# A two-layer decoder trunk on one core: the first weight block by halves, the variance product later, another order of the first value products, and more idle products

## The chip, the core and the metric

The kernel runs on one core of one Trainium2 chip. The metric is the device time of one execution in microseconds (us). Five engines work side by side, each on its own stream of instructions, and wait for each other by semaphores: TensorE (PE in the profile, its weight loads PEld), VectorE (DVE), ScalarE (ACT), GpSimd (POOL) and SyncE (SP), which here only issues DMAs.

## The reference

The input x has 512 tokens of 1024 numbers. Layer 0 is RMSNorm, one input projection, an attention of 8 heads with dilated windows beside a causal convolution of width 31 over 512 channels (its result goes through a LayerNorm over the channels and a swish), one output projection, a residual, and a mixture of experts. Layer 1 is RMSNorm, a retention of 4 heads (queries and keys 256 wide, values 512), its output projection, a residual and another mixture of experts. All of it is float32.

```python
u = rms_norm(h, mix_norm[layer])
h = h + mixer(u)                      # layer 0: attention + convolution; layer 1: retention
h = h + hierarchical_moe(rms_norm(h, ffn_norm[layer]), ...)   # top 2 of 32 experts, hidden 512
...
mu = jnp.mean(yf, axis=-1, keepdims=True)                     # LayerNorm of the convolution
var = jnp.mean(jnp.square(yf - mu), axis=-1, keepdims=True)
```

## The kernel before

**Products by parts.** Each float32 product of the projections is made of three products of a faster format: the high part of the data with the high part of the weights, the low part of the data with the high part of the weights, and the high part of the data with the low part of the weights. The tokens' parts are `uT_hi` and `uT_lo` (ACT copies the transposed rows out of PSUM, L1317, and DVE subtracts, L1676). The weights come in blocks of 2 MB into one of three slots of `raw`; ACT makes `w_hi` (`split_hi`, L652) and DVE `w_lo` (`split_lo`, L660), each in two halves of four of the eight slices of the contraction. A half is 128x2048 numbers. `dense_half` waits for the low part of a half (`lo_ok`) and then issues 12 products for each of four tiles (L816, L817, L818).

**The start.** SP loads x in four tiles of 128 tokens and then the blocks (L708, L702). ACT squares and takes roots, DVE scales (`norm`, L1653), PE turns each tile (`norm_tile`, L825, eight transposes, four to each half of the contraction), and ACT and DVE copy both halves of tile 0, then of tile 1, and so on. Only then does ACT split block 0, which it waits for as a whole.

**The attention.** 32 units (a tile of queries with a head) pass through a pipeline written out by hand: in step n PE makes the scores of unit n (L1145, with an idle product L1144 ahead), the transposes of unit n-2 (L1166) and the values of unit n-3 (L1176). DVE runs the convolution's taps beside it. The two products of the LayerNorm stand in this pipeline on PE: `cmean` in step 24 and `cvar` in step 30 (both L1159). `cvar` waits for three sums of the squares on DVE (`summed`, in step 29, L1771 to L1774), which wait for four squares on ACT (L1429). Behind it ACT takes a root (L1432), DVE a reciprocal (L1818), and a chain of ACT and DVE (L1833, L1410, L1413, L1827) makes the parts of the convolution's channels, which are the second half of the output projection's contraction. The output projection begins right behind the last unit.

**The routing of each layer.** Between the products of the router stand idle products (`warm`, L887, counts in `WARM`): 24 ahead of the product `slot_gate` (L973) and 8 behind it. PE then waits for the first gathered tokens (POOL's indirect DMA), turns them (L891), issues 14 more, and begins the experts: 32 a layer, each 72 products of 512 columns and 12 transposes.

**The first block of layer 1.** The values of head 0 come while DVE still adds the experts' rows tile by tile. The order on PE is: turn tile 0, half 0 of tile 0, turn tile 1, half 1 of tile 0, half 0 of tile 1, turn tile 2, half 1 of tile 1, half 0 of tile 2, turn tile 3, and the rest. Each of these halves waits for `w_lo` of its half. DVE waits for the rotary tables (`tab_r`, an ACT-queue DMA issued when the last tile has been turned) ahead of the first split of the next block, although only `rotate_heads` reads them.

## Time and profile before

| | |
|---|---|
| three runs | 1908.67, 1910.99, 1912.9 us (median 1910.99) |
| the profiled execution | 1912.56 us, its span 1910.8 us |
| PE busy | 1867.5 us, 98% of the span |
| DVE, ACT, POOL busy | 1473.1, 1092.4, 267.6 us |
| PE on the chain that ended last | 90%; DVE 5%, DMA 1%, ACT 1% |
| mean granted clock of TensorE | 0.992 |

The span is what the profiler saw of the program; the execution's time is 1.76 us more. The share of PE says that it decides, but a busy PE is not a fast one: its matmuls are pipelined, and it counts as busy at half its clock too. So the waits of PE and its clock, stretch by stretch, say more than the share.

### The profile page before, as it was taken

What the parts mean: (1) busy time and instruction counts of PE and PEld (TensorE: products, weight loads), DVE (VectorE), ACT (ScalarE), POOL (GpSimd) and SP (SyncE); (2) the same over time, 40 slices, a digit from 0 to 9 for tenths busy, and PEclk for the clock granted to TensorE, in tenths of its full rate; (3) what the DMA queues carried; (4) which work ended last, traced back from release to release, by engine and by line L of the source; (5) the groups of instructions that cost most, each with busy time, mean ns of one, the idle gap of its engine ahead of it and who ended that gap; (6) DMA issues with size and microseconds to landing.
All of it is one profiled execution on the core that took longest, in us unless ns stands there. A gap on an engine that the chain in (4) does not pass through costs nothing.

```text
span 1910.8 us, 23175 instructions
## 1 busy us (share of the span) xinstructions
PE 1867.5 (98%) x8791; PEld 1399.1 (73%) x8791; DVE 1473.1 (77%) x1384; ACT 1092.4 (57%) x1061; POOL 267.6 (14%) x136
## 2 busy tenths in 40 slices
PE   7999999999999999998999999999999999999997
PEld 5876787777777777777787777787777777777775
DVE  4999657889899899896443534367888989889988
ACT  4235536777777777774221312324777777777775
POOL 0020001222221222200000000000122122122120
PEclk9999999999999999999999999999999999999999
DMA  7521037999999999995222222214999999999996
GB/s 268 186 79 45 25 136 292 365 365 369 370 370 369 362 373 374 365 367 205 74 75 88 89 88 82 74 65 178 369 371 368 366 361 366 366 363 366 370 368 230
DMA packets 77532, 494.92 MB, mean 259 GB/s; under 512 B 14761, under 2 KB 27049, under 8 KB 52768
## 3 DMA queue, kind: packets, MB, share of 16 engines
q1 hardware_dynamic: 60512, 467.68, 65.3%
q0 software_dynamic: 13888, 16.26, 2.5%
q10 hardware_dynamic: 3072, 10.18, 1.5%
q8 instruction: 37, 0.61, 0.1%
q14 instruction: 23, 0.19, 0.0%
HBM read 492.53 MB, written 34.08 MB: 276 GB/s over the span
## 4 chain that ended last, share of the span: by engine, by line
PE 90%; DVE 5%; DMA 1%; ACT 1%; issue 1%; SPq 0%; DVEq 0%; ACTq 0%; POOLq 0%
PE psum L903 12%; PE psum L907 12%; PE psum L902 12%; PE psum L816 8%; PE psum L817 8%; PE psum L818 8%; PE psum L926 6%; PE psum L925 6%; PE psum L929 6%; PE psum L891 3%; PE psum L1256 2%; DVE xs L1708 2%; PE psum L916 1%; DVE w_lo L660 1%; PE psum L1145 1%
## 5 line engine op out<-in xcount | busy, mean ns | idle before, releaser
L673 DVE TENSOR_TENSOR w_lo<-raw,w_hi 128x2048 fp32r<-128x2048 f32 x384 | 863.1, 2288 | 119.3 <-ACT w_hi L683 117.6
L683 ACT ACTIVATE w_hi<-raw 128x2048 fp32r<-128x2048 f32 x384 | 713.7, 1911 | 30.5 <-DMA raw<-in_expert_w_up 18.6
L902 PE MATMUL psum<-w_hi,uT_hi 128*96 128x512 f32 x1024 | 404.8, 395 | 0.5 <-DVE uT_lo L1948 0.5
L903 PE MATMUL psum<-w_hi,uT_lo 128*96 128x512 f32 x1024 | 402.0, 393 | 0.0
L652 ACT ACTIVATE w_hi<-raw 128x2048 fp32r<-128x2048 f32 x46 | 87.9, 1913 | 336.7 <-PE psum L818 335.9
L907 PE MATMUL psum<-w_lo,uT_hi 128*96 128x512 f32 x1024 | 276.9, 392 | 0.0
L660 DVE TENSOR_TENSOR w_lo<-raw,w_hi 128x2048 fp32r<-128x2048 f32 x46 | 105.3, 2290 | 206.0 <-ACT w_hi L652 201.2
L2255 POOL DMA_INDIRECT y_dram<-y_e,index x60 | 131.5, 2191 | 828.5 <-DVE y_e L1965 785.4
L902 PEld LDWEIGHTS psum<-w_hi,uT_hi 128*96 128x96 f32 x1024 | 167.8, 164 | 66.0 <-DVE uT_lo L1948 0.8
L907 PEld LDWEIGHTS psum<-w_lo,uT_hi 128*96 128x96 f32 x1024 | 165.1, 161 | 69.6
L903 PEld LDWEIGHTS psum<-w_hi,uT_lo 128*96 128x96 f32 x1024 | 165.9, 162 | 66.2 <-issue 0.3
L2249 POOL DMA_INDIRECT x_e<-xs_dram,index x64 | 119.8, 1871 | 671.7 <-DVE index L1941 629.4
L925 PE MATMUL psum<-w_hi,uT_hi 128*96 128x512 f32 x512 | 203.9, 398 | 0.0
L926 PE MATMUL psum<-w_hi,uT_lo 128*96 128x512 f32 x512 | 200.7, 392 | 0.0
L816 PE MATMUL psum<-w_hi,uT_hi 128*128 128x512 f32 x352 | 139.6, 397 | 4.0 <-DVE uT_lo L1676 1.6
L929 PE MATMUL psum<-w_lo,uT_hi 128*96 128x512 f32 x512 | 138.1, 391 | 0.0
L817 PE MATMUL psum<-w_hi,uT_lo 128*128 128x512 f32 x352 | 138.1, 392 | 0.0
L818 PE MATMUL psum<-w_lo,uT_hi 128*128 128x512 f32 x352 | 137.9, 392 | 0.0
L1457 ACT ACTIVATE uT_hi<-psum 128x384 fp32r<-128x384 f32 x128 | 55.9, 489 | 130.4 <-PE psum L891 130.4
L816 PE MATMUL psum<-uT_hi,w_hi 128*128 128x512 f32 x256 | 102.0, 398 | 6.7 <-DVE w_lo L660 6.7
L929 PEld LDWEIGHTS psum<-w_lo,uT_hi 128*96 128x96 f32 x512 | 82.6, 161 | 34.9
L925 PEld LDWEIGHTS psum<-w_hi,uT_hi 128*96 128x96 f32 x512 | 84.4, 165 | 30.7
(220 smaller groups left out, 2301.9 us busy)
## 6 DMA issues: line engine op xcount, KB each, us to landing
raw<-in_expert_w_gate SPq DMA_DIRECT2D x64, 2048.0 KB, 9.9
raw<-in_expert_w_up SPq DMA_DIRECT2D x64, 2048.0 KB, 11.1
raw<-in_expert_w_down SPq DMA_DIRECT2D x64, 2048.0 KB, 10.1
raw<-in_odd_w_in SPq DMA_DIRECT2D x8, 2048.0 KB, 9.3
raw<-in_odd_w_in SPq DMA_DIRECT2D x8, 1024.0 KB, 7.8
raw<-in_odd_w_out SPq DMA_DIRECT2D x4, 2048.0 KB, 7.6
raw<-in_even_w_in SPq DMA_DIRECT2D x3, 2048.0 KB, 15.1
raw<-in_even_w_in SPq DMA_DIRECT2D x4, 1024.0 KB, 12.8
```

The lines of the kernel that those rows point to most:

```text
L673: nc.vector.tensor_tensor(part(w_lo[b]), src, part(w_hi[b]).bitcast(F32), ALU.subtract).then_inc(m.lo[b], 1)
L683: nc.scalar.activation(part(w_hi[b]), src, ACT.Copy).then_inc(m.hi[b], 1)
L816: nc.tensor.matmul(dst, still[0], moving[0], start=start, stop=False)
L817: nc.tensor.matmul(dst, still[1], moving[0], start=False, stop=False)
L818: return nc.tensor.matmul(dst, still[0], moving[1], start=False, stop=stop)
L902: nc.tensor.matmul(psum[0:r, bank], xeT_hi[:, c, 0:r], hi[:, j], start=(half + j == 0), stop=False)
L903: nc.tensor.matmul(psum[0:r, bank], xeT_lo[:, c, 0:r], hi[:, j], start=False, stop=False)
L907: mm = nc.tensor.matmul(psum[0:r, bank], xeT_hi[:, c, 0:r], lo[:, j], start=False, stop=(half * j == 3))
L925: nc.tensor.matmul(psum[0:r, bank + half], x[0][:, j, 0:r], hi[:, j], start=(j == 0), stop=False)
L926: nc.tensor.matmul(psum[0:r, bank + half], x[1][:, j, 0:r], hi[:, j], start=False, stop=False)
L929: mm = nc.tensor.matmul(psum[0:r, bank + half], x[0][:, j, 0:r], lo[:, j], start=False, stop=(j == HC - 1))
L2255: G.indirect_dma_start(y_dram, bass.IndirectOffsetOnAxis(ap=index[0:FIRST, 0, e, 1:2], axis=0), y_e[0:FIRST, b], None, bounds_check=TOPK * ...
```

## The change

- **First block by halves.** Block 0 comes in four DMAs rather than two: the first half of the contraction first, with a semaphore of its own (`first_landed`). ACT and DVE copy the first half of all four tiles, split the first half of the block, and then do the second halves.
- **Idle products at the start.** `START = (12, 4, 1, 1, 12)`: 12 products of 128x512 (bf16) ahead of the first transposes, 4, 1 and 1 between the tiles, 12 behind the last one (those wait until `uT_lo` of tile 0, half 0, is copied).
- **The variance product** moves from step 30 to step 34 on PE, the sums ahead of it on DVE from step 29 to step 31.
- **The first value products.** Tile 0 of the first block of layer 1: the 8 products with the high part of the weights of half 0 and of half 1, then the 4 with the low part of half 0, turn tile 1, the 4 with the low part of half 1. Then the tiles follow whole: tile 1, turn tile 2, tile 2, turn tile 3, tile 3. DVE copies tile 2 before it adds the last rows of tile 3, and waits for `tab_r` only ahead of `rotate_heads(0)`.
- **`WARM`** goes from 24 to 27 ahead of `slot_gate`, and from 8 to 12 behind it, in both layers.
- The semaphores of the rows (`x_in`, `y_in`) become one (`rows_in`), with the waits raised by 16.

```diff
-WARM = (46, 17, 24, 8, 14)
+WARM = (46, 17, 27, 12, 14)
+START = (12, 4, 1, 1, 12)
...
-        if n == CONV_AT + 8:
+        if n == CONV_AT + 12:
             b.plan(("cvar",), 3)
...
+            if (n, halves) == (0, (0,)):
+                act.wait_ge(first_landed, 32)
+            else:
+                act.wait_ge(landed[n % SLOTS], landed_at[n])
...
+                    if not n:
+                        for dst, src in ((slice(0, 256), gate_at), (slice(256, 512), value)):
+                            sp.dma_start(blocked(n)[:, 0:4, dst], w_in[:, 0:4, src:src + 256]).then_inc(first_landed, 16)
+                    j = slice(0 if n else 4, KC)
...
+            def idle_products(b, times):
+
+                for _ in range(times):
+                    nc.tensor.matmul(psum[:, b], idle_w[:, 0:P], idle_w, start=True, stop=True)
+
+            pe.wait_ge(idle_ok, 1)
+            idle_products(7, START[0])
             pe.wait_ge(ident_in, 16)
-            norm(0)
+            for q in range(TILES):
+                norm_tile(0, q)
+                if q < TILES - 1:
+                    idle_products(7, START[1 + q])
+            copied(pe, "norm", 0, 0, 0)
+            idle_products(banks.at("norm", 0, 0, 0)[0], START[TILES])
...
+                def first_tile(half, late):
+
+                    hi, lo = parts(pair_half(n, half))
+                    b, _, _ = banks.at(*names[0])
+                    if not late:
+                        if not half:
+                            open_bank(*names[0])
+                        pe.wait_ge(hi_ok[half], dense[n] + 1)
+                        copied(pe, "norm", 2, 0, half)
+                        for j in range(4):
+                            c = 4 * half + j
+                            nc.tensor.matmul(psum[:, b], uT_hi[:, c, 0:P], hi[:, j], start=(c == 0), stop=False)
+                            nc.tensor.matmul(psum[:, b], uT_lo[:, c, 0:P], hi[:, j], start=False, stop=False)
+                        return
+                    pe.wait_ge(lo_ok[half], dense[n] + 1)
+                    for j in range(4):
+                        mm = nc.tensor.matmul(psum[:, b], uT_hi[:, 4 * half + j, 0:P], lo[:, j], start=False,
+                                              stop=(half * j == 3))
+                    if half:
+                        mm.then_inc(bank_full[b], 1)
+
                 norm_tile(2, 0)
-                first_values(0, 0)
+                first_tile(0, False)
+                first_tile(1, False)
+                first_tile(0, True)
                 norm_tile(2, 1)
-                first_values(1, 0)
+                first_tile(1, True)
                 first_values(0, 1)
+                first_values(1, 1)
                 norm_tile(2, 2)
-                first_values(1, 1)
                 first_values(0, 2)
+                first_values(1, 2)
                 norm_tile(2, 3)
-                first_values(1, 2)
                 first_values(0, 3)
                 first_values(1, 3)
...
             norm(0)
-            for q in range(TILES):
-                copy_rows(0, q)
-            split_hi(act, 0)
+            for half in range(2):
+                for q in range(TILES):
+                    copy_rows(0, q, (half,))
+                split_hi(act, 0, (half,))
...
-                if n == CONV_AT + 7:
+                if n == CONV_AT + 9:
                     dve.wait_ge(csq_ok, BC)
                     summed(csq[:, 0], csq[:, 1], csq[:, 2], csq[:, 3], 1)
...
+                    copy_rows(2, 2)
                     add_last(3)
-                    copy_rows(2, 2)
                     norm(2, 3)
                     copy_rows(2, 3)
...
-            dve.wait_ge(tab_r_in, 16)
             cos_r, sin_r = tab_r[:, 0], tab_r[:, 1]
...
             lo("g", 0, 0)
+            dve.wait_ge(tab_r_in, 16)
             rotate_heads(0)
```

## Rows read from the trace of the kernel before

**Rows 1.** The waits of PE over the span: waiting line, releaser, us in total, times, longest.

```profile
PE psum L816 <- DVE w_lo L660: 7.8, 3, 5.2
PE psum L1159 <- DVE gain_row L1774: 3.0, 1, 3.0
```

**Rows 2.** Windows: busy us (x instructions) by engine, granted clock, DMA share, GB/s.

```profile
20.73:25.00 4.27, 4.27 (x10) 3.41 (x11) 2.27 (x2) 0.00 (x0) 0.00 (x0) 0.50 1.05 382
25.00:50.00 25.00, 25.00 (x111) 20.70 (x111) 6.78 (x6) 6.32 (x5) 0.00 (x0) 1.00 0.48 172
204.00:208.00 4.00, 4.00 (x18) 3.14 (x17) 0.50 (x3) 2.30 (x9) 0.00 (x0) 0.50 0.02 4
282.00:286.00 4.00, 4.00 (x22) 3.12 (x21) 1.99 (x3) 2.16 (x3) 0.96 (x1) 0.50 0.10 25
875.00:878.00 3.00, 3.00 (x8) 2.34 (x8) 2.96 (x5) 0.00 (x0) 0.00 (x0) 0.50 0.60 186
436.00:454.00 18.00, 18.00 (x87) 13.07 (x86) 16.26 (x12) 13.47 (x12) 3.07 (x2) 1.00 0.98 371
```

**Rows 3.** Timeline of the start: start us, us, engine line op, [idle before <-releaser].

```profile
10.79 4.79 PE L825 MATMUL psum<-square,xs 128*128 128x128 f32 x24 [0.21 <-DVE xs L1653]
12.23 1.28 DVE L1653 SCALAR_TENSOR_TENSOR xs<-h,stat,gain_row 128x1024 f32<-128x1024 f32 x1
11.86 4.40 ACT L1317 ACTIVATE uT_hi<-psum 128x512 fp32r<-128x512 f32 x8
16.44 1.91 ACT L652 ACTIVATE w_hi<-raw 128x2048 fp32r<-128x2048 f32 x1 [0.18 <-DMA raw<-in_even_w_in]
18.38 4.49 DVE L660 TENSOR_TENSOR w_lo<-raw,w_hi 128x2048 fp32r<-128x2048 f32 x2
20.73 0.80 PE L816 MATMUL psum<-uT_hi,w_hi 128*128 128x512 f32 x1 [5.15 <-DVE w_lo L660]
33.99 1.92 ACT L652 ACTIVATE w_hi<-raw 128x2048 fp32r<-128x2048 f32 x1 [13.84 <-PE psum L818]
```

**Rows 4.** Timeline, end of the attention and start of the output projection, three engines.

```profile
201.22 0.69 DVE L1774 TENSOR_TENSOR gain_row<-gain_row 128x512 f32<-128x512 f32 x1
202.06 1.56 PE L1159 MATMUL psum<-gain_row,square 128*128 128x512 f32 x2 [2.97 <-DVE gain_row L1774]
207.34 1.28 ACT L1432 ACT_TABLE_LOAD   x1
208.25 0.77 PE L816 MATMUL psum<-w_hi,uT_hi 128*128 128x512 f32 x1
209.35 3.35 DVE L1818 RECIPROCAL gain_row<-gain_row 128x512 f32<-128x512 f32 x1
220.10 0.69 DVE L1827 TENSOR_TENSOR uT_lo<-xs,uT_hi 128x512 fp32r<-128x512 f32 x1 [0.68 <-ACT uT_hi L1413]
```

**Rows 5.** Timeline of PE ahead of the experts, in layer 0 and in layer 1.

```profile
281.55 1.52 PE L891 MATMUL psum<-square,x_e 96*128 96x96 f32 x8 [0.85 <-DMA x_e<-xs_dram,index]
285.70 0.77 PE L902 MATMUL psum<-w_hi,uT_hi 128*96 128x512 f32 x1
1316.12 1.10 PE L891 MATMUL psum<-square,x_e 96*128 96x96 f32 x8 [0.78 <-DMA x_e<-xs_dram,index]
1317.06 1.15 PE L887 MATMUL psum<-count_w 128*128 128x256 bf16 x9
```

**Rows 6.** Timeline of the first blocks of layer 1, PE and DVE.

```profile
872.50 1.16 PE L825 MATMUL psum<-square,xs 128*128 128x128 f32 x8 [1.76 <-DVE xs L1653]
874.71 0.59 PE L816 MATMUL psum<-w_hi,uT_hi 128*128 128x512 f32 x1 [1.05 <-DVE w_lo L660]
880.18 1.29 DVE L1653 SCALAR_TENSOR_TENSOR xs<-h,stat,gain_row 128x1024 f32<-128x1024 f32 x1
897.00 2.29 DVE L660 TENSOR_TENSOR w_lo<-raw,w_hi 128x2048 fp32r<-128x2048 f32 x1 [4.65 <-DMA xs<-in_c_tab_r]
```

**Rows 7.** The page's list of the costliest groups: one row of ACT.

```profile
L683 ACT ACTIVATE w_hi<-raw 128x2048 fp32r<-128x2048 f32 x384 | 713.7, 1911 | 30.5 <-DMA raw<-in_expert_w_up 18.6
```

More of the change, by code:

```diff
@@ L436, in trunk_kernel @@
         landed = [sem(f"landed{s}") for s in range(SLOTS)]
-        x_in = [sem(f"x_in{q}") for q in range(TILES)]
+        first_landed = sem("first_landed")
+        rows_in = [sem(f"rows_in{q}") for q in range(TILES)]
         ident_in = sem("ident_in")
@@ L527, in trunk_kernel @@
         idle_ok = sem("idle_ok")
-        y_in = [sem(f"y_in{q}") for q in range(TILES)]
         moe_done = sem("moe_done")
@@ L645, in split_hi @@
             by_columns = n >= first_odd and odd_blocks[n - first_odd][0] == "wo"
-            act.wait_ge(landed[n % SLOTS], landed_at[n])
+            if (n, halves) == (0, (0,)):
+                act.wait_ge(first_landed, 32)
+            else:
+                act.wait_ge(landed[n % SLOTS], landed_at[n])
             for half in halves:
@@ L707, in _ @@
             for q in range(TILES):
-                sp.dma_start(h[:, q], x_dram[:, q]).then_inc(x_in[q], 16)
+                sp.dma_start(h[:, q], x_dram[:, q]).then_inc(rows_in[q], 16)
             for b in even_blocks:
@@ L716, in _ @@
                     value, gate_at = 3 * A_WIDTH + n * 256, 3 * A_WIDTH + B_WIDTH + n * 256
-                    fill(n, [(blocked(n)[:, :, 0:256], w_in[:, :, gate_at:gate_at + 256]),
-                             (blocked(n)[:, :, 256:], w_in[:, :, value:value + 256])])
+                    if not n:
+                        for dst, src in ((slice(0, 256), gate_at), (slice(256, 512), value)):
+                            sp.dma_start(blocked(n)[:, 0:4, dst], w_in[:, 0:4, src:src + 256]).then_inc(first_landed, 16)
+                    j = slice(0 if n else 4, KC)
+                    fill(n, [(blocked(n)[:, j, 0:256], w_in[:, j, gate_at:gate_at + 256]),
+                             (blocked(n)[:, j, 256:], w_in[:, j, value:value + 256])])
                 else:
@@ L756, in experts @@
                 sp.wait_ge(main.y_free, EXPERTS * (layer + 1))
-                load_rows(lambda q: y_in[q], (0, 1))
+                load_rows(lambda q: rows_in[q], (0, 1))
                 sp.wait_ge(main.down_psum, EXPERTS * (layer + 1) - 1)
-                load_rows(lambda q: y_in[q], (2, 3))
+                load_rows(lambda q: rows_in[q], (2, 3))
                 sp.wait_ge(index_ok, layer + 1)
@@ L1077, in gated_rows @@
                     c = slice(half * 512, (half + 1) * 512)
-                    pe.wait_ge(y_in[q], 32 * (layer + 1))
+                    pe.wait_ge(rows_in[q], 32 * (layer + 1) + 16)
                     pe.wait_ge(diag_ok, len(BY_PRODUCT[layer]) * TOPK)
@@ L1155, in _ @@
                     scores(n)
-                if n in (CONV_AT + 2, CONV_AT + 8):
+                if n in (CONV_AT + 2, CONV_AT + 12):
                     dst, full = open_bank("cmean" if n == CONV_AT + 2 else "cvar")
@@ L1308, in bank, with copy_rows @@
                 return psum[:, b], bank_free[b]
-            def copy_rows(n, q):
+            def copy_rows(n, q, halves=(0, 1)):
                 t = slice(q * P, (q + 1) * P)
-                for half in (range(2) if n % 2 == 0 else (1,)):
+                for half in (halves if n % 2 == 0 else (1,)):
                     src, free = bank("norm", n, q, half)
@@ L1324, in norm @@
                     if n == 0:
-                        act.wait_ge(x_in[q], 16)
+                        act.wait_ge(rows_in[q], 16)
                     elif n == 1:
@@ L1665, in last_norm, with copy_rows @@
                                            in1=gain_row[:, c], op0=ALU.mult, op1=ALU.mult).then_inc(xs_ready, 1)
-            def copy_rows(n, q):
+            def copy_rows(n, q, halves=(0, 1)):
                 t = slice(q * P, (q + 1) * P)
-                for half in (range(2) if n % 2 == 0 else (0,)):
+                for half in (halves if n % 2 == 0 else (0,)):
                     src, free = bank("norm", n, q, half)
@@ L1674, in copy_rows @@
                     if n % 2 == 0:
-                        dve.wait_ge(norm_hi, 2 * TILES * (n // 2) + 2 * q + half + 1)
+                        dve.wait_ge(norm_hi, 2 * TILES * (n // 2) + (2 * q + half if n else TILES * half + q) + 1)
                         V.tensor_tensor(uT_lo[:, c, t], src, uT_hi[:, c, t].bitcast(F32), ALU.subtract).then_inc(free, 1)
@@ L1684, in _ @@
                 norm(0, q)
-            for q in range(TILES):
-                copy_rows(0, q)
-            split_lo(dve, 0, 0)
-            split_lo(dve, 0, 1)
+            for half in range(2):
+                for q in range(TILES):
+                    copy_rows(0, q, (half,))
+                split_lo(dve, 0, half)
             V.memset(conv_in[:, :, 0:PAD], 0.0).then_inc(eps_ok, 1)
@@ L1988, in add_early @@
             def add_early(layer, q, choices=range(TOPK)):
-                dve.wait_ge(y_in[q], 32 * (layer + 1))
+                dve.wait_ge(rows_in[q], 32 * (layer + 1) + 16)
                 add_rows(q, gate_early, choices)
@@ L2035, in moe @@
                     for q in range(TILES):
-                        dve.wait_ge(y_in[q], 32 * (layer + 1))
+                        dve.wait_ge(rows_in[q], 32 * (layer + 1) + 16)
                     for k in range(TOPK * TILES):
```

## The prediction

> **What bounds the kernel now.** I read the page first (PE is busy for 98% of the span and is 90% of the chain that ended last), then the waits of PE, then its clock in windows, then the timelines around each wait. PE hardly waits: 7.8 us for `w_lo` in three places and once 3.0 us ahead of L1159 are the large ones behind the first transposes [rows 1]. So whatever gets PE past a wait, or gives it its clock back, moves the end, unless another engine is late a moment later. The clock matters as much as the waits: 10 products take 4.27 us at a granted 0.50 (1.2 GHz) and 111 take 25.0 us at 1.00 (2.4 GHz), so 0.43 against 0.23 us each [rows 2]. Each fall to 0.50 stands behind a stretch in which PE stood still or had little: at the start, at 204, at 282 and at 875 us [rows 2]. The change touches exactly these four. In the experts PE has no gap, 18.0 of 18.0 us [rows 2], so a gain ahead of them is not swallowed there.
>
> **Part 1, the start.** Now PE's last 24 transposes take 4.79 us, 0.20 each; at the full clock eight take 1.10 with the tail of the last, so about 0.12 each; ACT and DVE then copy eight parts (0.55 us each), and ACT splits at 16.44, when block 0 has landed, 0.18 us after it was free; DVE's first `w_lo` takes 2.25 us (half of 4.49), and PE starts at 20.73 [rows 3, 5]. After the change: the last scaled tile is ready at 12.23 + 1.28 = 13.5; its first four transposes end at 14.0 at the full clock; ACT's copy (0.55) ends at 14.6, `w_hi` (1.91) at 16.5, `w_lo` (2.25) at 18.8, PE starts at 18.9: 1.8 us earlier. The half block must have landed by 14.6. It has 1 MB less ahead of its end than the whole one, and at the 0.38 MB/us that the first window moves [rows 2] that is 2.8 us before 16.4, so 13.6. The two more DMA issues push block 1 back by about a microsecond; ACT wants it at 33.99 and idles 13.8 us before [rows 3]. Half 1 of block 0 (four copies, 1.9 and 2.25 us) is ready by 24, and PE has 48 products or 10.9 us of half 0. The idle products give the rest: 12 from about 1.5 us on (5.1 us at 0.43 each, against the ten products that PE did in the slow window before its clock rose [rows 2]), and 12 more between the last transposes and 18.9. With the full clock at 18.9 the ten slow products cost 2.0 us less. Sum 3.8 us. The other end: the clock stays at half throughout. Then 4, 1 and 1 idle products of 0.43 us push the tiles back, the last four transposes end at 16.8, the split chain at 21.5, and the last 12 idle products (5.1 us from 17.6) let PE go only at 22.7: 2.0 us lost. I take 3.8: in all four slow stretches the clock came back under steady products.
>
> **Part 2, the variance product.** PE arrives at `cvar` at 199.1, waits until 202.06 for the third sum (201.22 + 0.69), and is at half clock from there to the output projection at 208.25 [rows 2, 4]. That stretch is 6.2 us, 3.1 at the full clock. After the change PE runs on at 199.1. The three sums (0.69 each, partly overlapped) began at 199.9 and now come behind one more score and maximum, for which I estimate 0.8 us: 200.7 to 202.7. Meanwhile PE does the transposes and values of units 28 to 30, as fast as maximum, exponent and copy follow each other. So `cvar` still waits a little, at 202.7 instead of 202.06, but is now the last thing but one: with 1.1 us for it (1.56 at half clock in part [rows 4]) and the last values the output projection starts at 204.1. That is 4.2 us earlier, and its first four products at the full clock give 0.6 more: 4.8. What is late next: ACT's table load and root come behind `cvar`, so at 204 to 205.8; from the end of the root in the kernel before (209.3) to the last `cat_lo` (220.10 + 0.69) are 11.5 us [rows 4], so now 217.3. PE wants that part with half 1 of the projection, fourth slice: 204.1 + 48 products (10.9) + transposes (0.4) + nine products (2.0) = 217.4. The cover is 0.1 us, so a stall of some tenths is possible. The ends: if PE's clock falls again behind this thinner stretch, some ten products of the projection and its transposes cost 2.4 us, leaving 2.4; if in addition the sums take all of the old wait, 0; if nothing waits at all, 5.9.
>
> **Part 3, the idle products of the routing.** In layer 0 PE waits 0.85 us for the gathered tokens and the clock is at 0.50 behind it: the transposes take 1.52 us instead of 1.10, the fourteen idle products run from 283.1 to the first expert product at 285.70, and the first products are slow [rows 2, 5]. In layer 1 the same wait (0.78) leaves the clock up: transposes 1.10, fourteen idle products 1.69 [rows 5]. The seven new ones cost 7 x 0.12 = 0.84 us, just the wait that they fill, so nothing if the tokens don't land sooner. If they keep the clock in layer 0, the transposes save 0.6, the copies behind them then release PE at 284.5 instead of 286.0, and some five products save 0.2 each: 2.5 us. Ends: 2.5 gained; 0.8 lost in each layer, if the new products stand on the path. I take 2.5 in layer 0 and nothing in layer 1.
>
> **Part 4, the first block of layer 1.** Now PE waits 1.76 us for tile 1, turns it, waits 1.05 for `w_lo` of half 1 and starts at 874.71 at half clock until about 878.5; at 875 to 878 eight products take 3 us [rows 2, 6]. Tile 0 ends at about 879.2 (nine products at 0.43, three at 0.23). After: 8 + 8 + 4 products begin where the twelve of half 0 begin now (12 x 0.23 ahead of the wait that starts at 870.7, so at 867.9) and fill up to 872.5; tile 1 is turned to 873.4, and at 874.7 only four products are left of tile 0: it ends at 875.6, 3.6 us earlier. But most is given back. Tile 2 is scaled only at 880.18 + 1.29 = 881.5 [rows 6]. PE has 24 products (5.6 us) until 881.2, turns it until 882.4, and nothing stands behind it any longer: it waits some 0.9 us for ACT's and DVE's copy (0.55 and about 0.6). The same comes again with tile 3, turned at 889 to 889.9, 0.85 us. So 72 products, two turns and two waits end at 875.6 + 16.7 + 1.8 + 2.1, about 896.4, where now 72 products and the turns without a wait end at some 897.6. The next block's split waited for `tab_r` until 897.00 and ended at 899.3 [rows 6]; without that wait it follows ACT's `w_hi` and is done by 895.5, under the values. PE goes on at 896.4 instead of 899.3: 3.0 us. The tables are wanted only some 16 us later, which covers their landing. `add_last(3)`, now behind the copy of tile 2, delays tile 3's scaling from 887 to 888.2, still ahead of 889. Ends: clock falls as before, 1.1 gained; 3.6 with shorter waits.
>
> **Sum.** 3.8 + 4.8 + 2.5 + 3.0 = 14.1 us, off the profiled execution's 1912.56 (span 1910.8 and 1.76 around it): 1898.5. The median is 1.6 lower; I leave that out, as a run that escaped one slow-clock stretch has less to gain there. The merged semaphores cost nothing that I can find: each wait is for the same DMAs.
>
> **A rule that speaks against it.** Slow stretches of 2 to 4 us are in these rows at four places, and layer 1's router shows none where layer 0's does [rows 2, 5]. The Trainium skill ("TensorE: Matmul & The Clock Gate", Part 1: The HAM clock gate) says that the number of slow products at the beginning of a stretch differs from run to run of the same kernel. The trace agrees in so far as two equal stretches differ. By that rule a part of the clock's gain would be there in some executions only.
>
> **Rivals.** (a) *One or two stretches keep their slow clock*: `cvar`'s gives 2.4 instead of 4.8 and the start 3.0 instead of 3.8 (if the clock comes only during the transposes). 10.9 us, 1901.7. For it: the last units are thin work with small waits. Against it: the units ahead of 199 ran at the full clock in the same pattern. The Trainium skill's sentence cited above would bring this case in some executions. (b) *The clock's luck and the chains of copies eat more*: parts 1 to 4 at 3.0, 2.4, 0 and 1.1, so 6.5 us, 1906. (c) *The change does not do what it says*: idle products block the tiles, `cvar` waits as long, the clock falls all the same: between 0 and 3.8 us gained. (d) *Slower, by one mechanism*: the experts' loads. There the DMA share is 0.98 [rows 2] and ACT waited 18.6 us in all for landings of the up weights [rows 7], so far off the path. If a new phase between PE and the loads puts that wait on PE, it is -14.1 + 18.6 = +4.5 us: 1917. It decides from some 0.3 us per expert on. Against it: no load is issued but by a split, and splits follow PE, so all shift together.
>
> **Chances.** Forecast (1896 to 1900) 0.48; (a) 0.27; (b) 0.13; (c) 0.08; (d) 0.04. What a measurement here can tell from no change is 0.2%, 3.8 us. Forecast, (a) and (b) are faster, with a little of (c): 0.89; same 0.07; slower 0.04. The range takes the forecast's and (a)'s and half of (b): 1894.5 to 1904.5.
>
> **What would show it.** First real product at 18.9 and at 0.23 us spacing; no wait of 3 us at L1159 but one under 1 us, and the output projection's start earlier by what the start gained and another 4 to 5 us; a clock of 1.00 behind the gathered tokens of layer 0; in layer 1 two waits of about 0.9 us behind the second and third turned tile and none for `w_lo` of the next block. The prediction is wrong if PE's new waits at these places add up to more than 4 us, or if the clock is low behind any of the four.

## The result, and the profile after

| | before | changed |
|---|---|---|
| median, range | 1910.95 us, 1908.67 to 1912.9 (4 runs) | 1940.47 us, 1940.09 to 1943.62 (4 runs) |
| profiled execution, its span | 1912.56, 1910.8 | 1940.16, 1938.4 |
| mean granted clock | 0.992 | 0.976 |

The ratio is 1.0159, interval 1.0141 to 1.0176: the medians are 29.5 us apart, the changed kernel the slower one, where 1898.5 was predicted and the range ended at 1904.5. The runs further down showed that every version with the attention of the kernel before has executions of two kinds, some 37 us apart: the four of the changed kernel here are all of the slower kind, the four of the kernel before all of the other, so this ratio is the distance between the kinds and not the worth of the change.

PE is as busy as before, 98%. What differs on the page is its row of the clock (one digit for each fortieth of the span, 48 us; in the kernel before each digit is a 9):

```profile
span 1938.4 us, 23263 instructions
...
PE 1906.7 (98%) x8835; PEld 1419.4 (73%) x8835; DVE 1473.7 (76%) x1384; ACT 1092.5 (56%) x1061; POOL 264.6 (14%) x136
...
PEclk9995699999999999999999999999999999999999
```

The windows of PE (window; its length; busy us and instructions; granted clock; DMA share; GB/s) put the fall at 141 us and the return behind 226:

```profile
120.00:138.00 18.00, 18.00 (x80) 1.00 0.31 117
138.00:141.00 3.00, 2.23 (x11) 1.00 0.00 0
141.00:142.00 1.00, 1.00 (x9) 0.78 0.00 0
142.00:160.00 18.00, 18.00 (x51) 0.50 0.32 118
160.00:180.00 20.00, 20.00 (x68) 0.50 0.00 0
...
220.00:226.00 6.00, 6.00 (x19) 0.50 0.01 3
226.00:240.00 14.00, 12.72 (x70) 0.97 0.00 1
```

For 84 us PE runs at 1.2 GHz, and it is busy for all of it. The timeline of PE (start us; us; line, operation, tiles; in brackets the wait ahead) shows the place, steps 3 and 4 of the attention (line numbers are those of the kernel shown, so L1144 of before is L1164 here, L1145 is L1165, L1166 is L1186 and L1176 is L1196):

```profile
138.25 1.12 PE L1165 MATMUL psum<-kT,qT 64*128 64x512 f32 x2
139.30 0.66 PE L1186 MATMUL psum<-square,prob 128*128 128x128 f32 x4
140.73 1.19 PE L1196 MATMUL psum<-v,probT 128*128 128x64 f32 x8 [0.77 <-ACT probT L1467]
141.71 0.63 PE L1164 MATMUL psum<-idle_w 128*128 128x512 bf16 x1
142.27 2.07 PE L1165 MATMUL psum<-kT,qT 64*128 64x512 f32 x2
...
146.78 0.63 PE L1164 MATMUL psum<-idle_w 128*128 128x512 bf16 x1
```

Right behind the wait for the first transposed probabilities the products take twice as long, and a step takes 5.07 us (141.71 to 146.78). The kernel before has the same instructions and the same wait of 0.77 us at 143.89, and its step takes 2.69 us (144.81 to 147.50). The change touches nothing in these steps.

At the four places that the change is about the waits shrank, in this slow execution too. The waits of PE (line; releaser; us in total, times, longest) answer to [rows 1]:

```profile
...
PE psum L824 <- DVE uT_lo L1720: 3.6, 2, 2.5
PE psum L824 <- DVE w_lo L664: 1.8, 1, 1.8
...
PE psum L1237 <- DVE w_lo L664: 1.0, 1, 1.0
...
PE psum L1196 <- ACT probT L1467: 0.8, 1, 0.8
...
PE psum L1179 <- DVE gain_row L1818: 0.4, 1, 0.4
```

The 3.0 us at `cvar` are 0.4, the 7.8 us for `w_lo` are 2.8. A shorter wait is not yet a gain of that size: at the start the twelve idle products stand in the old wait, and the first real product comes at 19.56 us instead of 20.73. Only L824's 3.6 us for `uT_lo` are new, and larger than predicted.

### The profile page after: what moved, and what is told of

Its sections match the earlier page's. It is cut to its first block, busy times and chain, and to the rows that moved or that the text cites. A ratio compares the mean times of both kernels' runs of the same rounds, so it can differ in the third digit from the quotient of the medians.

```text
span 1938.4 us, 23263 instructions
## 1 busy us (share of the span) xinstructions
PE 1906.7 (98%) x8835; PEld 1419.4 (73%) x8835; DVE 1473.7 (76%) x1384; ACT 1092.5 (56%) x1061; POOL 264.6 (14%) x136
## 4 chain that ended last, share of the span: by engine, by line
PE 95%; DVE 3%; ACT 1%; issue 1%; DMA 0%; DVEq 0%; ACTq 0%; POOLq 0%
PE psum L911 12%; PE psum L915 12%; PE psum L910 12%; PE psum L824 9%; PE psum L825 8%; PE psum L826 8%; PE psum L934 6%; PE psum L933 6%; PE psum L937 6%; PE psum L899 3%; PE psum L1165 2%; PE psum L1299 2%; PE psum L924 1%; PE psum L1196 1%; PE psum L1186 1%; PE psum L833 1%
## 5 line engine op out<-in xcount | busy, mean ns | idle before, releaser
L687 ACT ACTIVATE w_hi<-raw 128x2048 fp32r<-128x2048 f32 x384 | 713.6, 1911 | 36.3 <-DMA raw<-in_expert_w_up 25.7
L911 PEld LDWEIGHTS psum<-w_hi,uT_lo 128*96 128x96 f32 x1024 | 165.5, 162 | 66.0
L824 PE MATMUL psum<-w_hi,uT_hi 128*128 128x512 f32 x344 | 135.4, 394 | 5.0 <-DVE uT_lo L1720 3.6
L825 PE MATMUL psum<-w_hi,uT_lo 128*128 128x512 f32 x344 | 134.0, 390 | 0.0
L826 PE MATMUL psum<-w_lo,uT_hi 128*128 128x512 f32 x344 | 134.0, 390 | 0.0
L934 PEld LDWEIGHTS psum<-w_hi,uT_lo 128*96 128x96 f32 x512 | 82.7, 162 | 31.0
```

The lines of the kernel that those rows point to most:

```text
L687: nc.scalar.activation(part(w_hi[b]), src, ACT.Copy).then_inc(m.hi[b], 1)
L824: nc.tensor.matmul(dst, still[0], moving[0], start=start, stop=False)
L825: nc.tensor.matmul(dst, still[1], moving[0], start=False, stop=False)
L826: return nc.tensor.matmul(dst, still[0], moving[1], start=False, stop=stop)
L911: nc.tensor.matmul(psum[0:r, bank], xeT_lo[:, c, 0:r], hi[:, j], start=False, stop=False)
L934: nc.tensor.matmul(psum[0:r, bank + half], x[1][:, j, 0:r], hi[:, j], start=False, stop=False)
```

## The experiments

An execution between 1938 and 1954 us is called a fallen one here, after the fall of the clock. The ratios compare executions that didn't fall; only for `fewer_idle`, `fewer_idle_burst` and `thin_two`, in which every execution fell, they compare fallen ones with undisturbed ones of the kernel before. The medians and ranges are over all executions. Differences in us are 1912 times the ratio's distance from 1.

| kernel | median us (range, runs) | ratio (interval) | fallen |
|---|---|---|---|
| before, beside them on four chips | 1911.62 to 1913.89 | 1 | 17 of 70 |
| no_part1 | 1906.34 (1904.15 to 1906.72, 6) | 0.9969 (0.9956 to 0.9982) | 0 |
| part1_only | 1909.49 (1906.16 to 1944.76, 10) | 0.9985 (0.9973 to 0.9997) | 1 |
| later_start | 1905.76 and 1903.92 | none | 0 |
| filled_stall | 1902.34 (1901.62 to 1903.06, 4) | 0.9949 (0.9933 to 0.9966) | 0 |
| changed_again | 1902.7 (1901.39 to 1904.66, 5) | 0.9949 (0.9935 to 0.9964) | 0 |
| before_filled | 1910.85 (1908.7 to 1919.09, 11) | 0.9991 (0.998 to 1.0003) | 0 |
| fewer_idle | 1943.89 (1942.69 to 1945.1, 2) | 1.0163 (1.0143 to 1.0183) | 2 |
| fewer_idle_burst | 1930.49 (1928.91 to 1932.08, 2) | 1.0093 (1.0073 to 1.0113) | 2, ended early |
| cvar_only | 1906.47 (1905.12 to 1946.23, 12) | 0.9974 (0.9964 to 0.9983) | 2 |
| warm_only | 1911.52 (1908.16 to 1949.74, 12) | 1.0001 (0.9991 to 1.001) | 2 |
| values_only | 1912.83 (1911.15 to 1950.29, 12) | 1.0006 (0.9997 to 1.0015) | 1 |
| changed_third | 1904.28 (1901.37 to 1940.09, 6) | 0.996 (0.9946 to 0.9974) | 1 |
| issues_later | 1900.79 (1900.14 to 1901.74, 6) | 0.9941 (0.9927 to 0.9955) | 0 |
| filled_again | 1903.69 (1900.7 to 1905.15, 6) | 0.9955 (0.9939 to 0.9971) | 0 |
| thin_two | 1939.99 (1938.04 to 1940.43, 4) | 1.0143 (1.0123 to 1.0163) | 4 |

**Is it the new start?** `no_part1` is the change without its first part, `part1_only` the first part alone, and `later_start` moves everything behind the start:

```diff
-START = (12, 4, 1, 1, 12)
+START = (12, 4, 1, 1, 35)
```

> The changed kernel without its first part (no START, block 0 as a whole), all other parts kept. Theory A (the loss is TensorE's clock, which falls to 0.50 at 141.8 us in the changed kernel, in step 4 of the attention, and stays there until 226 us; what moves the attention against the clock's own rhythm is part 1, the only part that acts before 141.8): the attention's first transposes are back at 140.7 us, the clock stays at 1.00 until 199 us, and the time is 1900 to 1905 us. Rival B (one of the later parts, the variance product or its bank, spoils the attention): still 1935 or more.

> The kernel before with part 1 alone (START and block 0 by halves). Theory A: the attention starts 3.2 us earlier than before (137.5) and the clock falls at about 141.8, as in the changed kernel; the old variance product is in it too, so the time is 1940 to 1952 us. Rival B: no fall, 1907 to 1909 us.

> The changed kernel with START = (12, 4, 1, 1, 35): 23 more idle products ahead of block 0, so PE begins it some 3.1 us later, and the attention comes at the time at which it came before the change (first transposes at 140.6 +- 0.2 instead of 137.5). Nothing else is different. Theory A in its narrow form (the same small stall of 0.8 us lets the clock fall or not by the time at which it comes): no fall, 1901 to 1905 us, so 36 to 39 us faster for 3 us of idle work. Rival C (the fall comes with the new order at the start, whatever its time: the halves, the four DMAs, a different course of DVE and ACT): it falls again, 1941 to 1946.

None of the three had the fall in its profile, so theory A failed on `part1_only`: its attention starts at 137.38 us, with the same wait, and the clock stays up. The kernel before, run beside them, had it in four of its 15 runs (1948.28 to 1953.11 us), `part1_only` in one of 10. So the fall does not belong to the new start, nor to the change: it comes with the single execution, in the kernel before too. (No fallen execution of the kernel before was profiled; its extra time, 36 to 41 us, and its mean clock in these runs, 0.968 to 0.973 against 0.989 to 0.996 in the others, are those of the fall.) (`later_start` had two more runs, of 2555 and 3772 us, disturbed by something else, the first at a mean clock of 0.68, the second at 1.0; it has no ratio.)

**Is it the wait of 0.77 us?** `filled_stall` puts three idle products into it, `before_filled` the same into the kernel before:

```diff
                         copied(pe, "v", TILES - 1)
+                        if n == VALUE_LAG:
+                            for _ in range(3):
+                                nc.tensor.matmul(o_dst, idle_w[:, 0:P], idle_w, start=True, stop=True)
```

> The changed kernel with three idle products (0.65 us) in step 3 of the attention, ahead of PE's wait of 0.77 us for the first probT. Theory D (the stall together with the thin steps around it is what lets the clock fall, so filling it keeps the clock): no fall at 141.8, 1898 to 1903 us. Rival E (the thin work of the attention is enough, the stall is not needed): the clock falls there or some us later, 1935 to 1942 us.

> The changed kernel once more, beside the kernel before, on one chip. In the runs so far the time of the kernel before was twice of two kinds, about 1908 to 1915 us and 1948 to 1953 us (4 of 15), so the fall of the clock in the attention may be a matter of the single execution. Theory F (every version with the unfilled stall falls in a part of its executions, and the first four of the changed kernel all did): of these runs some are at 1898 to 1903 us and some at 1940 to 1944. Theory A (the moment makes it certain): all at 1940 or more.

> The kernel before with the three idle products in step 3 of the attention and nothing else. Theory D and F: no execution at 1940 or more any longer, and the others as before, 1908 to 1915 us, within 1 us. If the stall is not what opens the way to the fall, some executions are still at 1948 to 1953 us.

The windows of PE in `filled_stall` have 2.97 busy us between 138 and 141 where the changed kernel had 2.23, and the clock stays up:

```profile
138.00:141.00 3.00, 2.97 (x16) 1.00 0.00 0
...
142.00:160.00 18.00, 17.08 (x101) 1.00 0.33 118
```

But `changed_again`, the changed kernel itself, was undisturbed as well in all of its five runs: its windows with the same 2.25 busy us and no fall are

```profile
138.00:141.00 3.00, 2.25 (x11) 1.00 0.00 0
...
142.00:160.00 18.00, 17.30 (x98) 1.00 0.33 118
```

so `filled_stall` alone shows nothing; it needed the count. And `changed_again` showed that the change is worth 0.5% when the clock stays up (0.4% in `changed_third`). `before_filled` had no fall in 11 runs, beside five in 15 of the kernel before, and is otherwise no faster. Two of its runs, 1917.16 and 1919.09 us, lie above the range expected; the trace of the latter has a wait of 2.8 us at L1071 where the kernel before has 0.8, and layer 0's experts take 577.4 us instead of 572.8. Why is open.

The wait of 0.77 us is one of two. Each undisturbed trace without the filling has a second one, of 0.7 us, 8.4 us later, and the filled ones keep it (0.76 and 0.77 us) and don't fall there. In `changed_again`:

```profile
149.46 0.63 PE L1186 MATMUL psum<-square,prob 128*128 128x128 f32 x4 [0.70 <-ACT prob L1435]
```

**Can the fall be forced, and what ends it?** `fewer_idle` takes the idle product out of five steps of the kernel before; `fewer_idle_burst` adds 25 in one piece in step 12.

```diff
-                if n >= AHEAD:
+                if n >= AHEAD and not 3 <= n <= 7:        # fewer_idle
+                for _ in range(0 if n < AHEAD or 3 <= n <= 7 else 25 if n == 12 else 1):   # fewer_idle_burst
```

> The kernel before without the idle product (L1144, 0.21 us each) of the attention's steps 3 to 7, so with less work for PE there. Theory D: the clock falls to 0.50 in these steps in every execution and does not come back until the sums of the squares or the output projection (226 us or later), although the later steps have their idle products again: 1942 to 1953 us. If the clock needs no such work to stay up: 1908 to 1914.

> The same with 25 idle products in one piece in step 12. Theory D, second half (the slow state keeps itself up, because at half clock the attention's steps are too thin for the clock to return, and only dense work ends it): the clock is back at 1.00 within the piece and stays up behind it; 8 us are paid for the piece and some 25 us of slow steps are saved: 1925 to 1937 us. If the slow state has another cause that lasts as long as it lasts, the clock stays at 0.50 through the piece: 1953 or more.

Both fell at 154 us in their profiles, and the times of all four runs agree with it. With the burst the clock is back at 177, without it at 222 (and it falls once more behind the old 3.0 us wait for the variance product, from 233 to 243; with the burst from 219 to 225). The windows of `fewer_idle_burst`:

```profile
145.00:154.00 9.00, 7.66 (x43) 0.99 0.29 90
...
160.00:177.00 17.00, 17.00 (x58) 0.50 0.00 0
...
178.00:200.00 22.00, 22.00 (x125) 1.00 0.00 1
```

and of `fewer_idle`:

```profile
160.00:180.00 20.00, 20.00 (x67) 0.50 0.00 0
180.00:200.00 20.00, 20.00 (x65) 0.50 0.00 1
200.00:221.00 21.00, 21.00 (x63) 0.50 0.00 0
221.00:234.00 13.00, 9.14 (x48) 0.89 0.00 1
```

The steps on both sides of the burst are the same work (they get smaller only as the attention goes on, from four blocks of keys to one), and the two kernels have the same steps there. At full clock this work keeps the clock (178 to 200 us); at half clock it does not get it back, though PE is then busy all the time. 25 dense products do it. Where nothing was put in, the clock came back behind `cmean`, two products of 512 columns, in each of the three kernels that show it: `cmean` starts at 223.13 us in the changed kernel, 221.86 in `thin_two` and 218.66 in `fewer_idle`, the clock is back at 226.9, 224.7 and 222.3.

The fall in these two kernels stands behind the second wait, not the first. Without the idle products both waits are longer: the first 0.99 instead of 0.77 us, behind which the clock stayed up, the second 1.34 instead of 0.7:

```profile
152.10 0.63 PE L1166 MATMUL psum<-square,prob 128*128 128x128 f32 x4 [1.34 <-ACT prob L1391]
```

So they show that thinner work forces the fall, but not whether by the missing work or by the longer wait.

**The sizes of the parts.** Parts 2, 3 and 4 alone on the kernel before, and the changed kernel once more.

```diff
-                if n in (CONV_AT + 2, CONV_AT + 8):       # cvar_only, with its two companions
+                if n in (CONV_AT + 2, CONV_AT + 12):
-WARM = (46, 17, 24, 8, 14)                                # warm_only
+WARM = (46, 17, 27, 12, 14)
-                first_values(0, 0)                        # values_only, with the order of the copies and the table wait
+                first_tile(0, False)
+                first_tile(1, False)
+                first_tile(0, True)
```

> The kernel before with the second part of the change alone: the variance product in step 34 instead of 30, its sums on VectorE in step 31 instead of 29. Theory (my prediction's part 2, with the size that the traces of the whole change gave): the stretch from the attention's first transposes to the output projection shortens from 67.6 to about 63.0 us, so the kernel takes 4 to 5 us less than before, a ratio of 0.9976, as long as TensorE's clock stays up in the attention. Rival (the next thing is late: the convolution's channels are not ready for the second half of the projection): PE waits inside the projection, and the gain is under 2.4 us. On the fall of the clock: if it were this part that brings it, its executions would lie near 1942 to 1948 in most cases; if the fall is open to every version, in some of them as in the kernel before (9 of 30).

> The kernel before with the counts of idle products in the routing alone: 27 instead of 24 ahead of the slot gate, 12 instead of 8 behind it. Theory (my prediction's part 3): layer 0 keeps its clock behind the gathered tokens, their transposes take 1.10 instead of 1.52 us, and the kernel takes 2.5 us less. The trace of the whole change says rather 1.0 us, from the gathered tokens to the first expert product 3.12 instead of 4.15 us. Rival (the seven new products stand on the path): up to 0.8 us a layer is lost, so 0 to 1.7 us slower. All three lie within 0.2%; the rows at the two places decide, not the time.

> The kernel before with the new order of layer 1's first value products, the copy of tile 2 ahead of the last addition, and the later wait for the rotary tables. Theory (my prediction's part 4): 3.0 us less. The trace of the whole change has a wait of 2.45 us behind tile 3 where I had 0.85, so about 1.5 us less is what I expect now. Rival (the order costs what it gives, the gain is all in the table wait): from the turning of tile 0 to the next block's first product the stretch stays within 0.5 us of the kernel before's, 34.2 us.

> The changed kernel once more, nothing altered, on whatever chip this is. Of its first nine executions four had the low clock in the attention (1940 to 1944 us, all on one chip), five had not (1901 to 1905 us, all on another). Theory (which of the two it is comes with the single execution, for any version with thin products in the attention): executions of both kinds, the low ones 1940 to 1944 and the others 1901 to 1905, in a share like that of the kernel before (9 of 30), with a profile of the one kind or of the other. Rival (the chip decides): all of one kind here, and the kernel before's runs beside it all of one kind as well. Rival (the change brings the fall): most of its runs low, few of the kernel before's.

In time `cvar_only` gains 5.0 us (3.3 to 6.9) and `part1_only`, on another chip, 2.9 (0.6 to 5.2); `warm_only` and `values_only` gain nothing that can be told (0.2 us and 1.1 us slower, with zero inside both intervals). Together that is 6.6 us, where the whole change gains 7.6 on this chip (5.0 to 10.3) and 9.8 in `changed_again` (6.9 to 12.4); the intervals are too wide to say whether the parts help each other. The rows that `warm_only` was to be read by went with its theory (transposes of 1.10 us), those of `values_only` fell between its theory and its rival: 33.51 us for the stretch instead of 34.24, 0.7 less. Both are taken up below. All four had executions of both kinds, and so had the changed kernel: one fallen run in six.

**What decides how often it falls, and the wait behind tile 3.** `thin_two` is the changed kernel without two idle products, `issues_later` the filled one with ScalarE's two DMA issues behind its copy of tile 3.

```diff
-                if n >= AHEAD:                            # thin_two
+                if n >= AHEAD and n not in (3, 4):
-            load_gain(3)                                  # issues_later, with the three idle products of filled_stall
-            act.dma_start(tab_r, c_tab_r).then_inc(tab_r_in, 16)
             copy_rows(2, TILES - 1)
+            load_gain(3)
+            act.dma_start(tab_r, c_tab_r).then_inc(tab_r_in, 16)
```

> The changed kernel without the idle products of steps 3 and 4 alone, two products of 0.23 us around the wait for the first transposed probabilities. Theory (how thin TensorE's work is around the wait sets how often the clock falls): most or all of the runs near 1940, where the changed kernel has 5 of 15; the runs without a fall at 1902 to 1904. Rival (the share of falls has nothing to do with the work in these steps, only the lack of idle products over five steps at a stretch did it in fewer_idle): about 1 run in 5 to 1 in 3 near 1940.

> The changed kernel with the three idle products once more, for the count. Theory (what the idle products cover is what lets the clock fall): 1901 to 1904 us in every run, none near 1940. Rival (chance: the fall comes in about 1 of 5 runs whatever stands in the stall, and 15 runs without it were luck, which happens in about 4 of 100): one or more of these runs at 1938 to 1941.

> The changed kernel with three idle products ahead of TensorE's wait for the first transposed probabilities (as in filled_stall), and with ScalarE's two DMA issues (the gain row, the rotary tables) behind its copy of tile 3 in layer 1 instead of ahead of it. Theory: the wait of 2.45 us behind the turned tile 3, where I had predicted 0.85, is made of these two issues, 0.35 and 0.45 us with gaps, that stand between the last transpose and ScalarE's copy: from 890.6 to 891.5 in values_only. So the wait becomes 1.2 us as behind tile 2, nothing waits for w_lo or the tables afterwards, and the kernel takes about 1.2 us less than filled_stall: some 1901. Rival: the tables or ScalarE's next split land late in turn, and a new wait takes what is won. On the fall of the clock: none in any run, as in the 15 runs with filled idle products so far.

`thin_two` fell in four runs of four. Its fall stands behind the first wait, which is longer here too, 0.99 instead of 0.77 us. The windows of its PE, and the row of the wait:

```profile
130.00:138.00 8.00, 8.00 (x39) 1.00 0.31 133
...
142.00:146.00 4.00, 4.00 (x15) 0.60 0.01 2
...
160.00:180.00 20.00, 20.00 (x64) 0.50 0.00 1
...
140.89 1.08 PE L1196 MATMUL psum<-v,probT 128*128 128x64 f32 x8 [0.99 <-ACT probT L1467]
```

Over all runs: with the first wait filled 0 of 27 fell (11, 4, 6, 6); with the wait as it is 28 of 143 (17 of 74 of the kernel before with the first four, 5 of 15 of the changed one, 6 of 54 of the parts and `later_start`); with two to five idle products fewer 8 of 8. At the rate of 28 in 143, 27 runs without one would come in about 3 of 1000 studies. (This takes 28 in 143 as exact and the executions as independent.) So what PE has to do around these waits sets how often the clock falls: two products fewer, or three more, are enough to change it. Fewer products also lengthen the waits and more shorten them; no run here changes the one without the other.

`issues_later` is the fastest version, 11.3 us below the kernel before (8.6 to 14.0), and its six runs lie within 1.6 us.

## Why the prediction was wrong

**The step that failed** is in the rivals, under (a): "the units ahead of 199 ran at the full clock in the same pattern". I read that row as a property of the kernel; it was one execution. The pattern at 141 to 145 us was visible in the trace of before, a wait of 0.77 us inside steps of thin work, and the list of PE's waits has it. I looked for slow stretches at the four places that the change touches and asked what the clock gives back there, never what it would cost if it fell at a place that the change leaves alone. The sum has no term for a fall elsewhere, that is, it puts it at nothing without a reason, and the largest loss among the rivals was (d)'s 4.5 us. The fall costs, in a step with all four blocks of keys, 5.07 instead of 2.69 us, and from 141.71 to the output projection 97.5 us (to 239.22) instead of 58.8 (141.94 to 200.78 in `changed_again`): 38.7 us, which is all of 1938.4 against 1900.9 and a little more. The prediction's own signs of being wrong did not catch it: the new waits come to 4.0 us (0.4 and 3.6), just its limit, and in the changed kernel's trace the clock is at 1.00 behind the gathered tokens.

Why the first four runs all fell, and none of the kernel before beside them, is open. Later 11 runs of the changed kernel on two chips had one. If every execution fell with the chance of 28 in 143, four of four would come in 15 of 10,000 such measurements; so it was a rare chance, or something that those runs shared, the chip or the hour, raised it, or the change does by an amount that 11 runs don't show. No run here tells these apart. What is shown is that the change is not needed for the fall and does not always bring it.

**By parts, in an undisturbed execution.** `changed_again` has a span of 1900.9, 9.9 us below the kernel before's, where I had 14.1; its 1902.7 us and `changed_third`'s 1904.28 lie inside the range given. The marks of PE in its trace, against [rows 3 to 6]; three engines, each in order of time:

```profile
...
10.16 1.91 PE L1120 MATMUL psum<-idle_w 128*128 128x512 bf16 x4
...
14.39 1.05 PE L833 MATMUL psum<-square,xs 128*128 128x128 f32 x8
...
15.53 1.90 ACT L656 ACTIVATE w_hi<-raw 128x2048 fp32r<-128x2048 f32 x1
...
17.46 2.29 DVE L664 TENSOR_TENSOR w_lo<-raw,w_hi 128x2048 fp32r<-128x2048 f32 x1 [1.04 <-ACT w_hi L656]
...
19.81 0.50 PE L824 MATMUL psum<-uT_hi,w_hi 128*128 128x512 f32 x1 [1.77 <-DVE w_lo L664]
...
199.70 1.10 PE L1179 MATMUL psum<-gain_row,square 128*128 128x512 f32 x2 [0.37 <-DVE gain_row L1818]
200.78 0.48 PE L824 MATMUL psum<-w_hi,uT_hi 128*128 128x512 f32 x1
...
273.55 1.10 PE L899 MATMUL psum<-square,x_e 96*128 96x96 f32 x8 [0.25 <-DMA x_e<-xs_dram,index]
...
282.34 1.02 PE L899 MATMUL psum<-square,x_e 96*128 96x96 f32 x8
```

- *Part 1, predicted 3.8, measured 2.9* (the attention's first transposes at 137.80 instead of 140.67). Products run at full rate from the first on, as said, and that gave 1.95 us of the 2.0 predicted (117.99 instead of 119.94 us from there to the attention). But the start is at 19.81, not 18.9: the twelve idle products end at 6.3 us, PE then waits 2.4 us for tile 0, and the clock was low behind it (0.58 from 8.7 to 11.6 us); the four behind tile 0 took 1.91 us, and so tile 3 was turned at 14.39 rather than 13.5. ACT's `w_hi` had the half block in time; the DMA term was right. In `changed_third` the same product starts at 20.98, so part of this gain changes with the execution.
- *Part 2, predicted 4.8, measured 4.6* (first transposes to output projection 62.98 us instead of 67.58), and 5.0 alone. The wait is 0.37 us, the clock stays up, and no stall shows in the second half: from the projection's start to the gathered tokens 72.8 us instead of 73.3.
- *Part 3, predicted 2.5.* From the gathered tokens' turn to that of the second expert 8.79 us pass instead of 10.75 (281.55 to 292.30 before), and with the shorter wait that is 2.5. The rows bear the mechanism out. In all ten traces with the new counts these transposes take 1.10 us and the stretch 8.69 to 8.80, in layer 0 and in layer 1. In the seven with the old counts the clock is low in layer 0 in six (transposes 1.33 to 1.52 us, stretch 9.25 to 10.78), `cvar_only` being the seventh (1.10 and 8.70), and in layer 1 in four. One row of each kind, `warm_only` with the new counts and `values_only` with the old:

```profile
280.07 1.10 PE L891 MATMUL psum<-square,x_e 96*128 96x96 f32 x8
...
281.67 1.52 PE L891 MATMUL psum<-square,x_e 96*128 96x96 f32 x8 [0.89 <-DMA x_e<-xs_dram,index]
```

What was mis-sized is the term: I took one execution's loss as what there is to gain. Over these traces the stretch is shorter by 1.1 us on average in layer 0 and by 0.4 in layer 1, where I had put nothing: an estimate of 1.6 us in all, which `warm_only`'s time neither shows nor excludes (from 1.7 us faster to 1.9 slower). Nine of the ten traces have the moved variance product too, and `cvar_only` kept the clock in layer 0 without the counts (in layer 1 it did not, 1.22 us); the counts alone stand on the one trace of `warm_only`, so how much of this is theirs is not shown. The term's own sum was high as well: the transposes save 0.42 us by [rows 5], not 0.6, and the first expert product comes at 285.70, not 286.0. The Trainium skill ("TensorE: Matmul & The Clock Gate", Part 1: The HAM clock gate) says that the count of slow products differs from run to run; the traces with the old counts agree, 8.70 to 10.78 us for the same work.

- *Part 4, predicted 3.0, measured 1.1* (turning tile 0 to layer 1's gathered tokens, 449.94 us instead of 451.02), and nothing alone. Other executions of the changed kernel scatter about this (452.00 in `changed_third`). From turning tile 0 to the next block the nine traces with this part as predicted have 33.06 to 35.07 us, the middle one 33.50, the seven without it 33.39 to 34.74, the middle one 34.24: 0.7 us. Tile 0 got its full clock and the wait for the tables was gone. Of the two waits predicted at 0.9 us, that behind tile 2 is 1.16, that behind tile 3 is 2.45. The missing term is ACT's. In `values_only`, the timelines of PE and of ACT:

```profile
...
889.57 1.04 PE L825 MATMUL psum<-square,xs 128*128 128x128 f32 x8
893.06 0.47 PE L816 MATMUL psum<-w_hi,uT_hi 128*128 128x512 f32 x1 [2.45 <-DVE uT_lo L1699]
...
890.64 0.35 ACTq L1368 DMA_DIRECT2D gain_row<-in_gains  x1
891.03 0.45 ACTq L1598 DMA_DIRECT2D xs<-in_c_tab_r  x1
891.52 1.08 ACT L1340 ACTIVATE uT_hi<-psum 128x512 fp32r<-128x512 f32 x2 [4.42 <-PE psum L825]
```

Two DMA issues, as soon as the tile is turned, stand ahead of the copy that PE waits for: 0.9 us. Before, the twelve products of tile 2 behind the turn hid them. With them behind the copy (`issues_later`) the wait is 1.57 us:

```profile
...
880.59 1.04 PE L833 MATMUL psum<-square,xs 128*128 128x128 f32 x8
883.21 0.47 PE L824 MATMUL psum<-w_hi,uT_hi 128*128 128x512 f32 x1 [1.57 <-DVE uT_lo L1723]
...
881.67 0.60 ACT L1363 ACTIVATE uT_hi<-psum 128x512 fp32r<-128x512 f32 x1 [3.54 <-PE psum L833]
881.67 0.35 ACTq L1391 DMA_DIRECT2D gain_row<-in_gains  x1
882.07 0.45 ACTq L1623 DMA_DIRECT2D xs<-in_c_tab_r  x1
```

I had expected 1.2; the 0.9 us that went are the issues' share. Its median is 2.9 us below `filled_again`'s on the same chip; two of these 2.9 are not explained by this wait, and `filled_stall` lay only 1.6 us above it on another chip.

The other cause of part 4 is its own order: without products of an earlier tile behind a turn, each copy's time falls on PE. `values_only` saves the next block's wait for `w_lo` (1.2 us in `cvar_only` and `warm_only`) and spends it there. An order that keeps products behind the turns together with the later table wait was not run. The last of the difference, 1.2 us, is lost in layer 0's experts (from the second expert to tile 0 of layer 1 574.0 instead of 572.8), 1.0 of it in one wait at L1079 that is shorter in another execution of the same kernel (1.71 us here, 0.75 in `changed_third`).

The rival (d), the experts' loads, did not come: the up weights' wait on ACT rose from 18.6 to 25.7 us in the changed kernel's page (17.6 in `changed_again`), and PE's waits list none of it.

## What to carry to other kernels

A wait of under 1 us on TensorE is cheap only as long as the clock survives it: where it lies in thin work, count what a fall would cost until the next dense stretch, and put a few idle products into the wait itself. A low or high clock seen in one trace is one draw; before a forecast counts it as gained or kept, it should be seen in several executions, and the gain be its average and not the one loss seen. A copy that comes to stand on the critical path brings everything ahead of it in its engine's queue along, DMA issues too.

## What the runs showed of the hardware

- TensorE's clock can stay at 0.50 for 84 us while the engine is 100% busy (142 to 226 us in the changed kernel); in another execution of the same kernel the same products keep it at 1.00 and take 46 us (142 to 188 in `changed_again`). The Trainium skill ("TensorE: Matmul & The Clock Gate", Part 1: The HAM clock gate) has activity release the throttle; here the trace shows a busy engine whose throttle is not released until `cmean`'s two products of 512 columns.
- 25 idle products in one piece end it (177 instead of 222 us, 13.4 us of time). With three in the wait, 0.7 us of work, none of 27 runs fell; with two fewer around it, and a wait of 0.99 instead of 0.77 us, four of four did.
- With 27 and 12 idle products around the product `slot_gate` (and, in nine of ten traces, the moved variance product) the transposes of the gathered tokens took 1.10 us in 20 of 20 places (ten traces, two layers), with 24 and 8 in 4 of 14; in the other ten 1.18 to 1.52, at the low clock in part or whole.
- `later_start` had one execution of 3772 us at a granted clock of 1.0: not every disturbance of a run is the clock's.
